# The first modulation in quarters instead of halves, the first projections by k-quarter behind it, and dense weights packed in their order of use

## The reference

```
c_act = silu(c)                                     # one vector of 1024
mod = c_act @ w_ada + b_ada                         # w_ada is 1024 x 3072
shift, scale, gate = split(mod, 3)                  # 1024 each
h = rmsnorm(x, norm_g) * (1 + scale) + shift        # 256 x 1024
proj = h @ w_in                                     # 1024 x 14344, read in blocks of 512 columns
...
```

## Time and profile before

| what | value |
|---|---|
| time, median of 3 runs (lowest to highest) | 1561.41 us (1560.77 to 1561.79) |
| span of the profiled execution, first to last instruction | 1556.7 us |
| TensorE busy | 1199.0 us, 77% |
| VectorE, ScalarE, GpSimd busy | 614.5, 426.0, 39.0 us |
| bytes moved by DMA | 550.51 MB, mean 354 GB/s |

### The profile page before, as it was taken

How to read it: one execution, slowest core, us unless ns; L and a number is a source line. 1 busy time by engine, 2 the same in 40 slices (tenths; PEclk the granted TensorE clock), 3 DMA queues, 4 the chain that set the end, 5 groups by cost and what they waited for, 6 DMA issues and landing times.

```text
span 1556.7 us, 18205 instructions
## 1 busy us (share of the span) xinstructions
PE 1199.0 (77%) x7368; PEld 694.3 (45%) x7368; DVE 614.5 (39%) x1041; ACT 426.0 (27%) x644; POOL 39.0 (3%) x64
## 2 busy tenths in 40 slices
PE   7999999999999999975665665675665666655675
PEld 6888977887887899621211111111111111111122
DVE  3786789889777877511011011011011011010111
ACT  3666357786564664300000000000000000000001
POOL 0100000010001000000000000000000000000000
PEclk9999999999999999988777777878877787788778
DMA  9877877686655666999999999999999999999996
GB/s 359 283 264 229 300 257 245 221 313 221 231 177 197 216 229 263 395 422 430 430 431 431 431 431 432 432 432 431 430 431 431 430 431 432 432 430 431 431 431 276
DMA packets 78195, 550.51 MB, mean 354 GB/s; under 512 B 5032, under 2 KB 5352, under 8 KB 61856
## 3 DMA queue, kind: packets, MB, share of 16 engines
q1 hardware_dynamic: 75024, 541.08, 86.0%
q0 software_dynamic: 2800, 7.97, 1.7%
q10 hardware_dynamic: 288, 0.30, 0.1%
HBM read 548.24 MB, written 1.61 MB: 353 GB/s over the span
## 4 chain that ended last, share of the span: by engine, by line
PE 46%; DMA 35%; DVE 12%; ACT 4%; issue 3%; DVEq 0%; ACTq 0%; POOL 0%; SPq 0%
PE ps L603 43%; DMA b<-in_w_down 34%; DVE b L1528 6%; PE ps L607 3%; ACT b L1164 3%; DVE b L1545 2%; DVE b L2258 1%; ACT b L1166 1%; DVE b L2199 1%; DMA b<-in_w_in 1%; DVE b L2205 1%; DMA b<-in_const 0%; DVE b L1538 0%; DVE b L1559 0%; DVE b L2239 0%
## 5 line engine op out<-in xcount | busy, mean ns | idle before, releaser
L603 PE MATMUL ps<-b,b 128*32 128x512 f32 (+7 forms) x6922 | 1129.9, 541 | 303.2 <-DMA b<-in_w_up 117.3
L603 PEld LDWEIGHTS ps<-b,b 128*32 128x32 f32 (+2 forms) x6922 | 637.6, 159 | 756.7 <-issue 450.1
L1164 ACT ACTIVATE b<-ps 128x512 f32<-128x512 f32 (+3 forms) x165 | 92.3, 559 | 874.9 <-PE ps L603 576.1
L1528 DVE TENSOR_TENSOR b<-b,b 128x1024 fp32r<-128x1024 f32 (+5 forms) x254 | 277.1, 1091 | 94.9 <-ACT b L1164 75.7
L1164 ACT ACTIVATE b<-b 128x1024 fp32r<-128x1024 f32 (+6 forms) x219 | 219.1, 1001 | 211.2 <-PE ps L603 164.5
L2248 DVE TENSOR_TENSOR b<-b,ps 128x512 f32<-128x512 f32 x16 | 11.0, 688 | 393.2 <-issue 379.9
L2258 DVE TENSOR_TENSOR b<-b,ps 128x1024 f32<-128x1024 f32 x28 | 34.2, 1222 | 311.2 <-PE ps L603 311.2
L607 PE MATMUL ps<-b,b 128*128 128x128 f32 (+1 forms) x360 | 70.0, 323 | 38.7 <-DVE b L1559 23.5
L607 PEld LDWEIGHTS ps<-b,b 128*128 128x128 f32 (+1 forms) x360 | 46.1, 169 | 89.1 <-DVE b L1559 36.4
L1545 DVE SCALAR_TENSOR_TENSOR b<-b,b,b 128x512 f32<-128x512 f32 (+3 forms) x50 | 63.2, 1263 | 4.3 <-ACT b L1164 0.5
L1528 DVE TENSOR_TENSOR b<-ps,b 128x512 f32<-128x512 f32 (+8 forms) x69 | 37.6, 545 | 27.4 <-PE ps L603 15.9
(11 more groups left out here) (60 smaller groups left out, 203.7 us busy)
## 6 DMA issues: line engine op xcount, KB each, us to landing
b<-in_w_gate SPq DMA_DIRECT2D x30, 4096.0 KB, 42.7
b<-in_w_up SPq DMA_DIRECT2D x30, 4096.0 KB, 43.2
b<-in_w_down SPq DMA_DIRECT2D x29, 4096.0 KB, 38.2
b<-in_w_in SPq DMA_DIRECT2D x73, 1024.0 KB, 5.4
b<-in_w_ada SPq DMA_DIRECT2D x28, 1024.0 KB, 5.3
b<-in_w_down SPq DMA_DIRECT2D x5, 2048.0 KB, 13.9
b<-in_w_ada SPq DMA_DIRECT2D x16, 512.0 KB, 11.4
b<-in_w_proj_m SPq DMA_DIRECT2D x8, 1024.0 KB, 5.3
```

The costliest lines, as they stand in the source:

```text
L603: return e.matmul(o, lhsT, rhs, start=start, stop=stop, skip_group_check=True)
L1164: e.activation(o, i, f, bias=bias, scale=scale).then_inc(mark[0], 1)
L1528: e.tensor_tensor(o, a, b, op).then_inc(mark[0], 1)
```

## The change

The first modulation is done in four quarters of two k-tiles' columns each: q0 ahead of g0, the others after g1, g4 and g7, each with one flip. The twelve first halves go quarter by quarter (V0, Q0, V1 of k-pair 0, then of k-pair 1, ...). On the host, the dense weights are packed into `dense` (one row of 8 KB per partition and load), the quarters of the modulation into `ada0`, the gate columns of `w_ada` into `ada_gate`, and two small tables likewise. The first 12 halves are loaded one by one. x is squared and scaled by ScalarE for one tile of tokens and by VectorE for the other, and the flipped x is copied out of PSUM by both. The eight modulation loads of TensorE move two slots later. The convolution of Q0 and the copies of V0 and V1 move with their inputs.

```
-            for i, (which, a) in enumerate((w, a) for a in (0, 2) for w in ("V0", "Q0", "V1")):
-                for j in range(2):
-                    add(which, a + j, a + j == 0, a + j == 3, (s + (2 * i + j) // 4, (2 * i + j) % 4))
+            for i, (a, which) in enumerate((a, w) for a in range(4) for w in ("V0", "Q0", "V1")):
+                add(which, a, a == 0, a == 3, (s + i // 4, i % 4))
...
-UNITS = [(g, ts) for g in range(NHALF - 2) for ts in (((0,), (1,)) if g == 4 else ((0, 1),))] + [(g, (t,)) for t in range(NT) for g in range(NHALF - 2, NHALF)]
+UNITS = [(g, ts) for g in range(NHALF - 2) for ts in (((0,), (1,)) if g in (2, 5, 8) else ((0, 1),))] + [(g, (t,)) for t in range(NT) for g in range(NHALF - 2, NHALF)]
...
-ADA_STEP = {(a + 1, 3): a for a in range(NADA_PE)}
+ADA_STEP = {(a + 3, 3): a for a in range(NADA_PE)}
...
@@ SyncE
+            def ada0(q):
+
+                for i in range(2):
+                    ks = slice(i * KD // 2, (i + 1) * KD // 2)
+                    src = dram["ada0"][q * P:(q + 1) * P, i * KD // 2 * W:(i + 1) * KD // 2 * W].rearrange("p (k n) -> p k n", n=W)
+                    e.dma_start(ADA0[q][:, ks, :], src).then_inc(S(f"ada0_{q}_{i}"), 16)
+            def first_half(g):
+
+                c, ks = g // 2, slice(2 * (g % 2), 2 * (g % 2) + 2)
+                if c >= RING:
+                    e.wait_ge(S("v_lo"), g - 2 * RING + 1)
+                e.dma_start(ring[c % RING][:, ks, :], dense(c)[:, ks, :]).then_inc(half_landed(g)[0], 16)
...
-            for k in range(0, KD, 2):
-                ada0(0, k)
-            ring_load(0)
-            ring_load(1)
-            for k in range(0, KD, 2):
-                ada0(1, k)
-                if k == 0:
-                    ring_load(2)
+            for q in range(4):
+                ada0(q)
+                for g in range(3 * q, 3 * q + 3):
+                    first_half(g)
...
@@ TensorE
-                    ins = mm(ps[32 * n:32 * n + 32, 7, 0:T], crep[:, k, :], ADA0[:, i, k, n * T:(n + 1) * T],
-                             k == 0, k == KD - 1)
+                    ins = mm(ps[32 * n:32 * n + 32, 7, 0:P], crep[:, k, :], ADA0[q][:, k, n * P:(n + 1) * P], k == 0, k == KD - 1)
...
             for k in range(KD):
                 ada0(0, k)
-                if k == 5:
-                    keep_clock(5)
-            ada0_flips(0)
+                if k == 3:
+                    keep_clock(6)
+            keep_clock(2)
+            ada0_flip(0)
             keep_clock(6)
...
-                if g == 4 and ts == (0,):
-                    for k in (4, 5, 6, 7):
-                        ada0(1, k)
-                if g == 4 and ts == (1,):
-                    ada0_flips(1)
+                if g in (2, 5, 8) and ts == (0,):
+                    ada0_flip(g // 3 + 1)
...
-                if (s, c) in ((0, 1), (0, 3)):
-                    for k in (c - 1, c):
-                        ada0(1, k)
+                if g in (1, 4, 7):
+                    for k in range(KD):
+                        ada0(g // 3 + 1, k)
...
@@ ScalarE
-            for t in range(NT):
-                act(XJ[:, t, :], X[:, t, :], ACT.Square, accum=csq[:, t:t + 1], to=S("a_xsq"))
-            for q in range(4):
+            act(XJ[:, 0, :], X[:, 0, :], ACT.Square, accum=csq[:, 0:1], to=S("a_xsq"))
+            e.wait_ge(S("g_pow"), 1)
+            act(XN[:, 1, :], X[:, 1, :], ACT.Copy, scale=csq[:, 1:2], to=S("a_xn"))
+            for q in (0, 2):
...
-                if (s, c) == (0, 3):
-                    e.wait_ge(*free("R0F1"))
-                    tokens_hi(2)
-                    tokens_hi(3)
+                if g in (2, 5, 8):
+                    tokens_hi(g // 3 + 1)
...
@@ VectorE
-                if (s, c) == (0, 2):
-                    modulation(1)
-                    tokens(2)
-                if (s, c) == (0, 3):
-                    modulate_lo("XT2", 1, HTL, HTH)
-                    tokens(3)
-                    modulate_lo("XT3", 1, HTL, HTH)
+                if g in (2, 5, 8):
+                    modulation(g // 3 + 1)
+                    tokens(g // 3 + 1)
+                    tokens_lo(g // 3 + 1)
```

More of the change, by code:

```diff
@@ L190 @@
 LOAD_AT = {what: i for i, what in enumerate(LOADS)}
+assert LOADS[:NFIRST // 2] == [("w", c) for c in range(NFIRST // 2)]
 CONTEXT_DONE, KEYS_DONE = (next(g // 2 for g in range(0, NHALF, 2) if HALVES[g][4] == (SLOT[n], 0)) for n in ("V2b", "CB"))
@@ L1662, in _ @@
             copy(crep2[:, :, 0:16], cst[:, KD:2 * KD].unsqueeze(2).broadcast_to([P, KD, 16]))
-            copy(crep2[:, :, 16:32], cst[:, 2 * KD:3 * KD].unsqueeze(2).broadcast_to([P, KD, 16]), to=S("v_crep"))
-            e.wait_ge(S("a_xsq"), NT)
+            copy(crep2[:, :, 16:32], cst[:, 2 * KD:3 * KD].unsqueeze(2).broadcast_to([P, KD, 16]), to=S("v_first"))
+            e.wait_ge(S("x_in"), 16)
+            e.wait_ge(*order.behind)
+            mark = order.mark(None)
+            e.scalar_tensor_tensor(out=XJ[:, 1, :], in0=X[:, 1, :], scalar=1.0, in1=X[:, 1, :], op0=ALU.mult, op1=ALU.mult,
+                                   accum_out=csq[:, 1:2]).then_inc(mark[0], 1)
@@ L1665, in _ @@
+            order.behind = mark
+            e.wait_ge(S("a_xsq"), 1)
             rstd(0, csq, D)
-            for t in range(NT):
-                ts(XN[:, t, :], X[:, t, :], csq[:, t:t + 1], None, ALU.mult, to=S("v_xn"))
+            ts(XN[:, 0, :], X[:, 0, :], csq[:, 0:1], None, ALU.mult, to=S("v_first"))
+            for q in (1, 3):
+                e.wait_ge(*full(f"XT{q}"))
+                copy(XTS[:, q, :], ps[:, 2 + q, :], to=free(f"XT{q}"))
             l4, neglam = lam4.rearrange("p (a b) -> p a b", a=4), lamv[:, 0:1]
-            def modulation(i):
-                e.wait_ge(*full(f"R0{i}"))
-                copy(MOD0[i], ps[:, 7, 0:T], to=free(f"R0{i}"))
-                e.wait_ge(*full(f"R0F{i}"))
-                v = ps[:, 6, 0:T].rearrange("p (b n j) -> p n b j", b=2, n=4)
-                gs, sh, bsc, bsh = (a[:, 4 * i:4 * i + 4].rearrange("p (n b) -> p n b", n=2) for a in (
-                    GS, SH, part(cols, COLS, "b_sc"), part(cols, COLS, "b_sh")))
-                tt(gs, v[:, 2:4, :, 0], bsc, ALU.add)
-                stt(GS[:, 4 * i:4 * i + 4], GS[:, 4 * i:4 * i + 4], 1.0, part(cols, COLS, "norm_g")[:, 4 * i:4 * i + 4], ALU.add, ALU.mult)
-                tt(sh, v[:, 0:2, :, 0], bsh, ALU.add, to=free(f"R0F{i}"))
@@ new lines, in modulation @@
+            def modulation(q):
+                e.wait_ge(*full(f"R0{q}"))
+                copy(MOD0[q], ps[:, 7, 0:P], to=free(f"R0{q}"))
+                e.wait_ge(*full(f"R0F{q}"))
+                v = ps[:, 6, 0:P].rearrange("p (n j) -> p n j", n=4)[:, :, 0]
+                gs, sh, bsc, bsh, gain = (a[:, 2 * q:2 * q + 2] for a in (
+                    GS, SH, part(cols, COLS, "b_sc"), part(cols, COLS, "b_sh"), part(cols, COLS, "norm_g")))
+                tt(gs, v[:, 2:4], bsc, ALU.add)
+                stt(gs, gs, 1.0, gain, ALU.add, ALU.mult)
+                tt(sh, v[:, 0:2], bsh, ALU.add, to=free(f"R0F{q}"))
@@ L1691, in _ @@
             lo(0)
[L1692 to L1694 removed]
+            tokens_lo(0)
             for g in (1, 2):
```

161 lines of the change are left out of this document (85 added, 76 removed).

## The result

| | median | lowest to highest | runs |
|---|---|---|---|
| before | 1560.77 us | 1559.3 to 1561.79 | 5 |
| with the change | 1566.06 us | 1564.41 to 1567.63 | 5 |

The ratio is 1.0039 (95% interval 1.0028 to 1.005): the change makes the kernel slower by 5.3 us, more than the 3.1 us that can be told from none. The forecast was 1563.4, its own range ended at 1565.5, the whole range at 1567.5. So the time is inside the range only because the range took in the rivals, and it is on the side to which I had given 0.30.

A forecast was written before the change was run, and what follows sets the result against it. The dense part was taken as bound by one TensorE stream. Terms -2.4 + 1.3 + 1.8 + 0.1 + 0.4 + 0.75 = +1.95 us moved the span from 1556.7 to 1558.7; plus 4.7 gave 1563.4, range 1558.5 to 1567.5.

The forecast's parts named there:

- the rivals: Whole kernel: small records no shorter 1570.7, new waits 1565.7, ring starving near 1567; faster, DMA deciding the experts' start, 1557.9.
- the side to which I had given 0.30: Whole kernel: the outcome "slower", chance 0.30, beside faster 0.16 and same 0.54.
- term 1.3: Head: const lands later, its rows sharing DMA engines with 8 KB rows behind x; +1.3 us, bounds 0 and 1.8.
- term 1.8: Modulation: 64 records of 128 columns at 28 ns take 1.8 us; -1.8 in the head, +1.8 in the stream.
- the rival of 57 ns: Modulation: small records get no shorter; +1.8 in the head, +5.5 in the stream, 1570.7 us; chance 0.07.
- the head's terms: Up to g0: modulation, identity matmuls, flip and ScalarE wait together 2.4 us sooner, const 1.3 later.
- A wait of 0.25, three times: +0.75: After the flips in g2, g5, g8: TensorE waits 0.25 us for the 1.9 us chain through VectorE and ScalarE.
- flips of +0.1: TensorE's stream: three single flips instead of two in a row cost +0.1 us.
- the new waits reach 1.0 each: Behind the later quarters' flips: VectorE's queued low parts lengthen the waits; +2.3 us, 1565.7; chance 0.11.
- Cost 0: Slots 9 and 10: two buffers hold modulation loads at once, yet 8.9 us remain for a landing of 5.3.
- The rival that had 0.06: Slots 9 and 10: the ring starves, +4.4 us less what the waits hide, near 1567; chance 0.06.
- The packed loads save DMA time that nobody waits for: Dense weight loads: packing was counted as hidden, with no term in the sum.

The follow-up runs named there:

- every repair: The changed kernel with even modulation loads, const first with 19 identity matmuls, quarters one half earlier: 1558.95 us (rows of 8 KB), 1559.70 us (rows of 2 KB).

## Why the prediction was off by 2.7 us

**Right.** `const` later by 1.2 (term 1.3): it landed after 7.6 to 8.4 us in the executions with the change that have it on ScalarE's queue, after 6.7 and 6.1 in the two without. The size is as said; that the rows of 8 KB behind x are the cause is argued, for no run changed these rows alone. Records with 128 columns: 32 in 1.08 us with the tail of the last, a block of 64 with its switches 1.89 us (term 1.8); so the rival of 57 ns falls. x by two engines: nothing. The three in-stream blocks, 5.67 us against 3.86 for the 64 records of before: +1.8, as said. g0 started 0.82 sooner where the head's terms gave 1.1. The experts kept 431 GB/s, and no wait of TensorE for data came before 60 us.

**Wrong, first: "A wait of 0.25, three times: +0.75", with flips of +0.1.** From g0's start to the gates block TensorE needed 42.9 us (64.58 - 21.66) where before needed 39.5 with a modulation block of 1.0 us in it, 38.5 without. That is +4.4, and 1.8 of it is records. 0.8 was lost in g0 and g1 (from g0 to the first block 6.85 us, before 6.05), for which I had 0.4. The other 1.8 is flips and stops, for which I had 0.85. With the quarters one half earlier 2.3 of these 2.6 us went. The chain behind the flip was sized rightly (1.9, measured 2.03). I took the cover too long: one token tile at 1.4 us plus 0.23, where the tile's six weight loads were done after 1.23. The flip's own switch, the two stretches in which weight loads stood (0.38 and 0.39 around the first product), and the first product alone between them came on top. So a quarter cost 0.6 where I had 0.28, and the rival "the new waits reach 1.0 each" was not reached. The half of 2.84 us in the prediction has the gates block in its mean; g8 to g11 alone took 2.78 each.

**Wrong, second: "Cost 0" for the ring at slots 9 and 10.** The rival that had 0.06 is what happens, and its sign, a wait for DMA near slot 9, came (VectorE's and ScalarE's). TensorE stopped for 0.6 to 1.3 us and not for 4.4, in all five executions with these places. I had taken the landing of 5.3 us for the worst load; where three loads were issued within 4 us, the last took 12.2, while I had put 13.3 down as the other end only.

**Not foreseen: the packed weights' price**, +1.4 us on before by the time (interval 0.3 to 3.0). "The packed loads save DMA time that nobody waits for" was half right: nobody waits for the saved time. In the one trace all of it that is not the clock is near 330 us, where a kernel with unpacked weights lost nearly as much (1.8 against 2.1). How much is the rows, and how much the chance of the execution, was not separated.

The sum of the terms as measured: +3.6 to the gates block (4.4 less the 0.8 of the head), +0.7 to 1.4 for the ring, and up to 1.4 for the packing, 4.3 to 6.4, against 5.3 in the medians. Between the two profiled executions stand besides the clock near 479 us (1.6), up to 2.4 near 336 and 348, and 0.9 in the experts, which no run explains.

**What stays open.** What makes the granted clock fall for some 3 us in the dense part in one execution and not in the next; whether ctx is what holds up the dense load near 320 us; and what of the packing's cost is from rows.

## What to carry to other kernels

A piece of work cut into smaller ones is paid for at each cut: the matmuls cost what their columns cost, but each cut brought a chain through two other engines, and here it was hidden only with a whole half between its start and its use. Place it one stage ahead before judging the cut. Before moving work earlier, find what starts the engine at all: here a table of 192 KB in a second queue held the head, and neither smaller pieces nor a second engine for x could show their worth until it was first. Even then, with every repair, the whole change came out level with the kernel before. Where two loads of a ring of four are put side by side, take as landing time the one behind a full queue (12.2 us here, against 5.3). And check the one profile of before against its median before reading a place of it as the rule.

## What of the hardware was not expected

With `const` first the granted clock fell in the head at 11.9 us, behind 2.6 us of idle TensorE (8.2 to 10.8 us), and rose again by 15.4; it stayed at 1.00 when 18 more identity records filled the gap. The stretches of the two kernels from 12.0 to 15.3 us:

```profile
12.00:15.30 3.30, 3.30 (x40) 2.49 (x38) 1.27 (x2) 1.71 (x3) 0.00 (x0) 0.50 1.00 392
```

```profile
12.00:15.30 3.30, 3.30 (x58) 2.81 (x60) 1.18 (x2) 1.65 (x2) 0.00 (x0) 1.00 1.02 395
```

By the Trainium skill (TensorE: Matmul & The Clock Gate, "Part 1: The HAM clock gate") the clock is throttled unless TensorE is active. In the head the traces agree.

Inside the dense part, with TensorE busy for 458 of 464 us ahead of it, the clock fell for 3.4 us; such falls stand in ten of fourteen executions, at 1.5 to 1.6 us each. Near 479 us a stop of 1.95 us stands just ahead; near 127 us TensorE waits for nothing. The four executions without a fall have the same stop, so the stop alone does not decide it. One execution of each of two kernels can therefore not show a difference of that size.
